# Two more pairs of w_up tiles a layer as seven block products; one SiLU and two small copies in another place

## The reference

```python
        h = rmsnorm(x, p["ffn_norm"][layer])
        up = h @ p["w_up"][layer]
        c, fb = causal_dwconv(up, ffn_bufs[layer], p["ffn_conv_w"][layer], p["ffn_conv_b"][layer])
        x = x + (jax.nn.silu(c[..., :D_FF]) * c[..., D_FF:]) @ p["w_down"][layer]
        new_ffn.append(fb)
```

## Time and profile before

| | |
|---|---|
| runs (3) | 1163.71, 1164.00, 1164.05 us; median 1164.0 |
| profiled execution | 1163.62 us |
| its span (first to last instruction) | 1161.9 us |
| TensorE busy | 1145.3 us (99%), 8442 matmuls |
| VectorE busy | 818.0 us (70%) |
| GpSimd busy | 722.1 us (62%) |
| ScalarE busy | 580.0 us (50%) |
| mean DMA rate | 90 GB/s |
| mean granted TensorE clock | 0.998 of full |

### The profile page before, as it was taken

How to read it: one execution, slowest core, us unless ns; L and a number is a source line. 1 busy time by engine, 2 the same in 40 slices (tenths; PEclk the granted TensorE clock), 3 DMA queues, 4 the chain that set the end, 5 groups by cost and what they waited for, 6 DMA issues and landing times. The chain is left out here.

```text
span 1161.9 us, 21843 instructions
## 1 busy us (share of the span) xinstructions
PE 1145.3 (99%) x8442; PEld 1124.9 (97%) x8442; DVE 818.0 (70%) x1506; ACT 580.0 (50%) x1113; POOL 722.1 (62%) x691
## 2 busy tenths in 40 slices
PE   8999999999999999999999999999999999999997
PEld 8887999999999999999999999999999999999997
DVE  5999768878677867775614644388686778678655
ACT  7475555544554555453613533366346545654543
POOL 3996344359867985872564324334698679768633
PEclk9999999999999999999999999999999999999999
DMA  6311242203421422131422222322042213232312
GB/s 233 117 56 36 67 146 81 93 28 95 142 65 44 149 73 92 56 137 51 149 84 91 69 69 74 117 82 65 28 147 91 80 61 116 74 92 80 120 51 82
DMA packets 35688, 104.01 MB, mean 90 GB/s; under 512 B 5105, under 2 KB 7153, under 8 KB 35569
## 3 DMA queue, kind: packets, MB, share of 16 engines
q1 hardware_dynamic: 31504, 98.92, 26.9%
q10 hardware_dynamic: 4080, 3.69, 1.1%
HBM read 98.29 MB, written 4.79 MB: 89 GB/s over the span
## 5 line engine op out<-in xcount | busy, mean ns | idle before, releaser
L594 PE MATMUL psum<-x_hi,w_hi 128*128 128x320 f32 (+2 forms) x1564 | 336.4, 297 | 1.3 <-POOL w_lo L1664 1.3
L594 PE MATMUL psum<-x_lo,w_hi 128*128 128x320 f32 (+2 forms) x1564 | 334.8, 295 | 0.0
L594 PE MATMUL psum<-x_hi,w_lo 128*128 128x320 f32 (+2 forms) x1564 | 334.1, 295 | 0.0
L1664 POOL TENSOR_TENSOR w_lo<-w_raw,w_hi 128x1024 fp32r<-128x1024 f32 (+1 forms) x84 | 181.8, 2169 | 188.0 <-ACT w_hi L1041 188.0
L594 PEld LDWEIGHTS psum<-x_hi,w_hi 128*128 128x128 f32 x1564 | 258.8, 188 | 3.6 <-POOL w_lo L1664 1.6
L594 PEld LDWEIGHTS psum<-x_hi,w_lo 128*128 128x128 f32 x1564 | 258.5, 188 | 0.0
L594 PEld LDWEIGHTS psum<-x_lo,w_hi 128*128 128x128 f32 x1564 | 257.3, 188 | 0.0
L2412 DVE SCALAR_TENSOR_TENSOR psum<-arena,params,psum 128x608 f32<-128x608 f32 x176 | 150.4, 854 | 58.8 <-ACT psum L1420 55.8
L1806 POOL TENSOR_TENSOR w_lo<-arena,w_hi 128x384 fp32r<-128x384 f32 x120 | 130.8, 1109 | 49.6 <-ACT w_hi L1331 49.6
L839 PE MATMUL psum<-block_hi,w_lo 128*128 128x288 f32 x504 | 149.2, 296 | 0.0
L839 PE MATMUL psum<-block_hi,w_hi 128*128 128x288 f32 x504 | 149.2, 296 | 0.0
(11 more groups left out here) (270 smaller groups left out, 2207.1 us busy)
## 6 DMA issues: line engine op xcount, KB each, us to landing
w_raw<-in_w_up SPq DMA_DIRECT2D x44, 512.0 KB, 3.7
arena<-in_w_up SPq DMA_DIRECT2D x44, 512.0 KB, 4.3
arena<-in_w_down SPq DMA_DIRECT2D x24, 384.0 KB, 3.6
w_raw<-in_w_down SPq DMA_DIRECT2D x24, 384.0 KB, 3.2
w_raw<-in_w_in_c SPq DMA_DIRECT2D x16, 512.0 KB, 3.5
w_raw<-in_w_in_ab SPq DMA_DIRECT2D x11, 512.0 KB, 3.6
w_raw<-in_w_out_ab SPq DMA_DIRECT2D x16, 256.0 KB, 2.7
w_raw<-in_w_out_c SPq DMA_DIRECT2D x8, 512.0 KB, 3.6
```

Of the source, the lines that this page charges most:

```text
L594: last = nc.tensor.matmul(PS[:, 2 * (q % 2 if slot is None else slot) + half, 0:b - a], w[q][:, k * P:(k + 1) * P], r[:, r_at, a:b], start ...
L1664: nc.gpsimd.tensor_tensor(w_lo[slot][:, 0:nk * P], raws[RAW_SLOT[RAW[u]]][:, 0:nk * P], w_hi[slot][:, 0:nk * P].bitcast(F32), ALU.subtract ...
```

## The change

The fifth pair of group 0 and the third pair of group 3 become seven-product pairs, in both layers (six a layer in place of four). In every seven-product pair ScalarE's SiLU goes behind the first taps of both tiles; where another such pair follows it would be put off behind that pair's first bank copy. GpSimd's two pads of such a pair go from the front of the pair's work behind the fifth step of its weights. By the pattern, three things follow that the diff does not show: `AHEAD` splits the weights of the new pairs and of their neighbours as seven products, `tokens_cut` cuts the pairs ahead of them at 288 columns, and the weight sums of the new pairs are made in the pairs ahead of them. A seven-product pair takes eight halves of `w_hi` and `w_lo` in place of four, so the halves of what follows shift by four.

```diff
--- before.py
+++ after.py
@@ -49,7 +49,7 @@
     KH = DH // P
     KF = w_down.shape[3] // P
     GROUPS = ((0, 6), (6, 6), (12, 6), (18, KF - 18))
-    PATTERN = ("PPPPPP", "PPSPSP", "PPSPSP", "PPPP")
+    PATTERN = ("PPPPSP", "PPSPSP", "PPSPSP", "PPSP")
     PB = state_pool.shape[2]
     CB = state_conv.shape[2]
     TAPS = CB + 1
@@ -1462,14 +1462,17 @@
                         for n in range(1, 7):
                             if n in (1, 2, 3, 5):
                                 bank_copy(layer, g, i, PAIR_ORDER[n - 1])
+                            if n == 1 and after_s(g, i):
+                                silu(i - 1)
                             weights_hi(layer, g, AHEAD[g][(h, i), n])
                             if n == 3:
                                 (blocks_hi if FAST[g] else product_hi)(i - 1)
                             if n == 5 and FAST[g]:
                                 block_sums_hi(i - 1)
                         tap0(i, 0, u + 3)
-                        silu(i)
                         tap0(i, 1, u + 8)
+                        if not following_s(g, (h, i)):
+                            silu(i)
                     if FAST[g]:
                         copy_p1(ud, 0)
                         for m in range(5, 8):
@@ -1909,10 +1912,11 @@
                                 weights_lo(layer, g, AHEAD[g][(h, i), j])
                                 keep_rows(t, j, u + j + 1)
                             continue
-                        pad(t, 0)
-                        pad(t, 1)
                         for n in range(7):
                             weights_lo(layer, g, AHEAD[g][(h, i), n])
+                            if n == 4:
+                                pad(t, 0)
+                                pad(t, 1)
                             if n == 1:
                                 for name in sums:
                                     pair_weight_sum(layer, h, i + 1, name)
```

## The result

The changed kernel takes 1166.05 us (median of 20 executions, 1163.68 to 1168.08), the one before 1163.92 in the same comparison (20, 1163.54 to 1165.92): a ratio of 1.0016, 95% interval 1.001 to 1.0022. It is slower by 2.1 us where I forecast 1.8 us faster.

The account below looks back on a forecast made before the run. TensorE, busy 99% at its upper clock, was taken as the bound. Group 3's -3.00 and group 0's +1.18 (waits of 2.09 less gains of 1.50) gave -1.82 us: 1162.2 from 1164.0, range 1161.2 to 1163.0, chance 0.70.

Parts of the forecast that it names:

- 0.70 for R4: Ahead of group 0's fifth pair, VectorE's R4 weight sum, 0.77 long, delays the evacuation by 0.70 us.
- wait (sum less 3.21): In group 0's new pair PE wants S2 3.21 behind the pair's start but waits 2.09 us for it.
- the second rival: Group 0's fourth pair: GpSimd's and VectorE's sums slow each other, wait 3.63, +1.26 us, 1165.3; chance 0.06.
- the argument against it: S1 and S2 took 1.29 in group 1 beside VectorE's taps, which read one operand from PSUM; so 1162.2.
- A clock that fell in the new wait would also cost: PE's clock in group 0's new wait: the longest wait so far, 1.7 us, left it up; counted as nothing.
- my own 0.4 and 1.7: Group 0's new wait of PE, split by S1's 1.6 us of matmuls into about 0.4 and 1.7 us.
- 12.74 - 11.24 = 1.50: Each of four changed pairs drops 12 matmuls, gaining 1.50 us; 6.00 us in all with no new wait.
- Group 3's two pairs: Group 3's third pair, both layers: no new wait, margin 0.37, both gains kept whole, -3.00 us.
- 0.59 behind GpSimd's sums: Group 0: ScalarE is free at 791.50, not 790.91, behind GpSimd's sums, moving the pair's chain by 0.59 us.
- 0.07 for the third evacuation instruction: Ahead of group 0's new pair, the cut at 288 columns makes the evacuation 0.89 in place of 0.82 us.
- 0 for the SiLU, the pads, the weights and the loads: Seven-product pairs: moved SiLU and pads, weight splitting and loads neither gain nor cost PE time, 0 us.
- my own bound of 2.3 us: A measurement of this kernel tells 0.2%, 2.3 us, from no change; chance of landing within it 0.71.

Follow-up runs that it names:

- group 3 alone: Changed kernel with group 0 plain again and group 2's fifth pair plain too, so only group 3's seven-product pairs are new: 1163.91 us, ratio 1.0003.
- old_pattern: Changed kernel with the pair pattern of before, keeping only the moved SiLU and pads: 1163.92 us, ratio 1.0002.
- late_early: late_r4, with GpSimd making the fifth pair's S1, S2 and R3 sums in group 0's third pair, ahead of its last row copies: 1159.20 us, ratio 0.9957.
- late_r4: Changed kernel with R4's sum behind the second tile's evacuation and ScalarE's first bank copy ahead of R4's split: 1159.98 us, ratio 0.9967.
- R4's sum on GpSimd: Changed kernel with R4's weight sum made by GpSimd, not VectorE, fourth in its row, for all seven-product pairs: 1161.47 us, ratio 0.9977.
- the sixth pair: Changed kernel with group 0's seven-product pair as the sixth in place of the fifth, both layers: 1163.02 us, ratio 0.9994.
- sum_late: Changed kernel with R4's sum behind the second tile's evacuation, ScalarE's split of R4 still ahead of the bank copy: 1161.52 us, ratio 0.9984.
- S1 twice: Changed kernel with PE computing group 0's S1 product twice, 12 more matmuls in the time of the wait for S2: 1164.76 us, ratio 1.0009.
- pattern_only: Kernel before with the new pair pattern alone, SiLU and pads in their old places: 1166.38 us, ratio 1.0025.
- group 0 alone: Changed kernel with group 3 plain again and group 2's fifth pair plain too, so only group 0's seven-product pairs are new: 1173.72 us, ratio 1.007.

## Why the prediction was wrong

Two steps failed, and the first term of the sum was 0.4 too large; the others held.

**The term "0.70 for R4".** Layer 1's rows against the steps as I set them up, counted from the pair's start (796.72 then, 797.42 now):

| step | predicted | measured |
|---|---|---|
| pair's start to R4's sum | 1.91 | 799.26 - 797.42 = 1.84 |
| R4's sum to the evacuation | 0.70 | 800.98 - 799.26 = 1.72 |
| evacuation, three instructions | 0.89 | 801.86 - 800.98 = 0.88 |
| its end to S2 | 1.80 | 803.74 - 801.86 = 1.88 |
| wait (sum less 3.21) | 2.09 | 3.11 |

All of the miss is in the second row. I took the duration from group 1, where the sum at 878.52 had only the last 0.23 us of GpSimd's operation to wait for and came ahead of the next one (878.70), so that GpSimd paid (1.75 in place of 1.29). In group 0 GpSimd's operation begins 0.03 us ahead of the sum, in both layers, and VectorE waits for nearly all of it: 1.80 in place of 0.77. The order is no accident: ScalarE's last sums of x (797.36, 1.27) release both the last sums of VectorE, behind which R4's sum stands, and ScalarE's own high part of R3, whose end (799.15) releases GpSimd. The prediction had R3's low part at 799.9, 3.2 behind the pair's start and so behind R4's sum; it began 1.8 behind it (799.23). The prediction does not ask what releases it.

So the second rival named the right mechanism, and R4's sum too, which it had at 1.38 (+0.61); it measured 1.80 (+1.02 to the next start). Its larger part, 0.92, it gave to GpSimd's sums S1 and S2, and those took 1.30 and 1.28 us (788.35, 789.83), as was argued there from the taps' operand in PSUM. Its 1165.3 is near the measured time by luck: the waits and the matmuls give 1164.6 (the account below), and the clock the rest. What failed is the argument against it: it clears S1 and S2 and then takes 1162.2 for the whole, though R4's sum itself reads two operands from SBUF, which is the very case that the rule quoted there is about. The Trainium skill ("SBUF — State Buffer", section "SBUF: two separate sides") says that the port pair of the two engines is an exclusive lock for a whole instruction, taken by whichever starts first. The trace agrees: 0.54 or 0.55 from GpSimd's end to the sum's end, whenever the sum was started.

**"A clock that fell in the new wait would also cost … I count nothing for it."** It fell. My reason was that a wait of 1.7 us had left the clock alone. The new one is 0.5 and 2.6 us with 1.6 us of matmuls between. The cost was written down as a condition and given no chance. What no run shows is whether the clock would have stayed up at my own 0.4 and 1.7; the nearest ones, 0.5 and 0.9 to 1.1, kept it up in 29 of 32 executions.

| kernel | waits ahead of S1, S2 (us, by the issue times) | executions at 0.997 or less | median us |
|---|---|---|---|
| before | none | 3 of 70 | 1163.9 |
| group 3 alone | none | 2 of 11 | 1163.91 |
| old_pattern | none | 2 of 11 | 1163.92 |
| late_early | none, 0.4 | 0 of 5 | 1159.20 |
| late_r4 | 0.5, 0.4 | 0 of 6 | 1159.98 |
| R4's sum on GpSimd | 0.5, 0.9 | 0 of 11 | 1161.47 |
| the sixth pair | none, 0.6 | 1 of 11 | 1163.02 |
| sum_late | 0.5, 1.1 | 2 of 10 | 1161.52 |
| S1 twice | 0.5, 1.0 | 1 of 11 | 1164.76 |
| changed kernel | 0.5, 2.6 | 13 of 20 | 1166.05 |
| pattern_only | 0.5, 2.6 | 9 of 11 | 1166.38 |
| group 0 alone | 0.5, 2.6 | 3 of 5 | 1173.72 |

A few executions are slow in the clock whatever the kernel; with the long wait it is most of them. The median executions of the changed kernel, at 0.996 or 0.997, carry about one fall of 1.5 us (1164.6 + 1.5 = 1166.1).

**The term 12.74 - 11.24 = 1.50.** 12.74 is the plain pair that stands ahead of a seven-product pair, with its second unit cut at 288. Other plain pairs take 2 x 6.35 = 12.70 (82.50 for 13 units; 25.39 for two pairs at 812.01). A changed pair was one of these, and the pair ahead of it became one of the former: 12.70 to 11.24 and 12.70 to 12.74, so 1.42 by these rows. Layer 0's group 3 shows the net of it: from its second pair's first matmul to layer 1's first product of line L594, PE took 578.18 - 505.58 = 72.60 before and 578.88 - 507.69 = 71.19 now, so 1.41 less.

**What held.** Group 3's two pairs at 11.24 without a wait; 0.59 behind GpSimd's sums (0.52 by the table's first row); 0.07 for the third evacuation instruction; the waits' places and releasers; 0 for the SiLU, the pads, the weights and the loads.

**The account.** With four times 1.41, -5.6 + 6.23 = +0.6, against a median that is 0.7 above that of before with the clock up; the falls bring it from 1164.6 to 1166.05. PE's first matmuls of the stages say the same: groups 0 to 2 take 1.74 more in layer 0 and 1.78 in layer 1, group 3 and what follows 1.41 and 1.39 less, +0.72 in all. The profiled execution lost 0.37 more ahead of layer 0's FFN. That does not belong to the change: 0.31 of it lies in the stage from 76 to 99 us, which took 22.31 before, 22.62 here, and between 22.26 (`sum_late`) and 22.79 (R4's sum on GpSimd) in kernels with the same work up to there. With R4 at 1.72 and 1.41 for a pair my sum would have been 1164.6, no change by my own bound of 2.3 us; most of what makes the kernel slower is the clock.

Open stays what decides between a fall and none: the same kernel shows both, and in one execution one layer and not the other. `late_r4` changes two things, and it is `sum_late` that tells their shares.

## What to carry to other kernels

Where a VectorE instruction reads two operands from SBUF, look up which GpSimd instruction is under way or released at the same moment, and which comes first: the second one pays the rest of the first. A duration from a row is only as good as that order. A new wait of TensorE longer than any that the trace shows can have a second price in its clock, to be put in the forecast with a chance; where the wait could not be removed, useless matmuls in it were worth 1.3 us more than idleness here.

## What the runs showed of the hardware

- A 128x512 float32 sum of two SBUF tiles on VectorE takes 0.68 us with no GpSimd operation beside it. Beside one it ended 0.54 or 0.55 behind GpSimd's end, whenever it began: 1.80 us when a GpSimd operation of 1.28 began 0.03 ahead, 1.60 at 0.24 ahead, 1.01 at 0.81 ahead. The other way round GpSimd's 1.29 becomes 1.75. Even a 128x18 copy on GpSimd went from 0.22 to 0.68 behind VectorE's sum. VectorE's evacuation from PSUM (0.45) and its taps (0.85) beside the same GpSimd work kept their times.
- Behind waits of 0.5 and 2.6 us TensorE's clock fell from 2.4 to 1.2 GHz in most executions (25 of 36), for about 3 us, 1.5 us of time each; with 12 more matmuls of 0.13 us in the wait, 10 of 11 executions stayed at 0.998 or 0.999. The same kernel shows a fall behind one wait and none behind an equal one.
